# The feed-forward part's first chunk: its up tiles become a Strassen quad, with the block sums begun in rows 6 and 7

## What is computed

```
hn = rms_norm(x, g_pre_ffn)
gu = hn @ w_gate_up                       # 1024 x (2 * 2816)
hf = silu(gu[..., :2816]) * gu[..., 2816:]
ff = hf @ w_down                          # 2816 x 1024
x  = x + rms_norm(ff, g_post_ffn)
```

## Time and profile before

| what | value |
|---|---|
| median of 3 runs | 1764.18 us (1764.01 to 1764.57) |
| the profiled execution: its own time | 1763.94 us |
| its span, first to last instruction | 1762.4 us |
| TensorE busy | 1752.1 us (99%) |
| VectorE busy | 1132.3 us (64%) |
| ScalarE busy | 733.2 us (42%) |
| mean granted TensorE clock | 0.999 of full |

### The profile page before, as it was taken

One profiled execution on the slowest core, in us unless ns is written; L12 is line 12 of the kernel. 1 busy time (PEld: TensorE's weight loads), 2 busy tenths in 40 slices (PEclk: granted clock), 3 DMA queues, 4 the chain that ended last, 5 costly groups with the idle time before them and its releaser, 6 DMA issues.

```text
span 1762.4 us, 23988 instructions
## 1 busy us (share of the span) xinstructions
PE 1752.1 (99%) x8497; PEld 1453.7 (82%) x8497; DVE 1132.3 (64%) x1927; ACT 733.2 (42%) x1486; POOL 249.7 (14%) x555
## 2 busy tenths in 40 slices
PE   9999999999999999999999999999999999999998
PEld 7888888888888888888888888888888888888886
DVE  5328888888775774443555655776656655567676
ACT  5316666666643233343221123343333333344553
POOL 3321222222210001111100112101011000000011
PEclk9999999999999999999999999999999999999999
DMA  7421222222143223337635712223233322673443
GB/s 244 144 85 57 76 74 73 73 73 72 49 144 95 72 66 130 104 102 259 219 132 167 240 60 83 96 96 142 93 111 109 105 89 102 228 279 100 145 143 126
DMA packets 138047, 213.80 MB, mean 121 GB/s; under 512 B 7569, under 2 KB 94097, under 8 KB 136930
## 3 DMA queue, kind: packets, MB, share of 16 engines
q1 hardware_dynamic: 109200, 108.54, 19.6%
q0 software_dynamic: 28752, 104.04, 16.2%
q10 hardware_dynamic: 2, 0.00, 0.0%
HBM read 150.17 MB, written 62.39 MB: 121 GB/s over the span
## 4 chain that ended last, share of the span: by engine, by line
PE 98%; DVE 1%; ACT 1%; DMA 0%; issue 0%; POOL 0%; POOLq 0%; DVEq 0%; ACTq 0%
PE ps L2343 26%; PE ps L2678 22%; PE ps L2546 17%; PE ps L2734 12%; PE ps L2427 10%; PE ps L2351 3%; PE ps L2443 3%; PE ps L2465 2%; PE ps L2467 1%; DVE ring L1564 0%; DMA x_tile<-in_x_dram 0%; ACT e_t L1089 0%; ACT ring L968 0%; DVE e_t L1667 0%; DVE d_op L1564 0%
## 5 line engine op out<-in xcount | busy, mean ns | idle before, releaser
L2734 PE MATMUL ps<-d_op 128*128 128x512 f32 x924 | 210.3, 389 | 0.1
L2734 PEld LDWEIGHTS ps<-d_op 128*128 128x128 f32 x924 | 173.3, 188 | 36.8 <-DVE d_op L1564 0.5
L2678 PE MATMUL ps<-s_op,t_op_T 128*128 128x512 f32 x720 | 169.9, 389 | 0.0
L2427 PE MATMUL ps<-xn,ring 128*128 128x512 f32 x672 | 167.0, 398 | 0.0
L2678 PEld LDWEIGHTS ps<-s_op,t_op_T 128*128 128x128 f32 x720 | 135.1, 188 | 28.1
L2427 PEld LDWEIGHTS ps<-xn,ring 128*128 128x128 f32 x672 | 122.3, 188 | 24.2
L2546 PE MATMUL ps<-s_op,x_op_T 128*128 128x512 f32 x576 | 135.9, 389 | 0.0
L2546 PEld LDWEIGHTS ps<-s_op,x_op_T 128*128 128x128 f32 x576 | 108.1, 188 | 22.5
L2678 PE MATMUL ps<-hn,t_op_B 128*128 128x512 f32 x480 | 115.1, 389 | 0.0
L2678 PEld LDWEIGHTS ps<-hn,t_op_B 128*128 128x128 f32 x480 | 90.1, 188 | 18.7
L1676 DVE CUSTOM_DVE_ANT_0 ps<-ps,mask 128x256 f32<-128x256 f32 (+7 forms) x128 | 94.5, 780 | 12.2 <-PE ps L2443 11.1
(11 more groups left out here) (270 smaller groups left out, 3361.4 us busy)
## 6 DMA issues: line engine op xcount, KB each, us to landing
pair<-in_w_gate_up_dram SPq DMA_DIRECT2D x20, 1024.0 KB, 5.2
rf_pieces<-s_scratch SPq DMA_DIRECT2D x74, 256.0 KB, 2.6
x_pair<-in_w_in_dram SPq DMA_DIRECT2D x16, 1024.0 KB, 6.7
raw<-in_w_in_dram SPq DMA_DIRECT2D x26, 512.0 KB, 4.0
s_scratch<-gated_ff POOLq DMA_DIRECT2D x40, 256.0 KB, 2.5
gate_in<-gate_scratch POOLq DMA_DIRECT2D x18, 512.0 KB, 3.6
v_scratch<-v_out POOLq DMA_DIRECT2D x32, 256.0 KB, 2.6
vh<-v_scratch POOLq DMA_DIRECT2D x16, 512.0 KB, 5.1
```

What stands on the lines that cost most here:

```text
L2427: last = pe.matmul(ps[:, proj_bank(first, half), :], proj_weights(which, par, a)[:, P * k:P * (k + 1)], xn[:, b, k, HALF * half:HALF * (ha ...
L2678: last = pe.matmul(ps[:, bank, :], t_op[name][:, a, k, :], block(b, k), start=opens and (k, a, b) == (0, HH, HH), stop=(k, a, b) == (3, LL ...
L2734: last = pe.matmul(ps[:, DOWN_BANKS[product][i], :], d_op[:, g % 4, a, P * i:P * (i + 1)], d_op[:, g % 4, 2 + b, :], start=opens and (a, b ...
```

## The change

The first chunk's four direct up groups go (`GROUPS = G_FFN + 4`); a kind-1 quad stands in their place, the first of 21. The first chunk's gate groups stay, in the order tile 0, tile 1 of the first half, then of the second, and their silu goes straight into `gated_ff`. The DRAM detour, `first_sums`, the `silu` and `hf_raw` tiles go; POOL stores chunk 0 as any other. VectorE adds hn's blocks earlier: `w00` in row 6, `w10` and 256 columns of a third block in row 7, 128 and 384 columns behind row 7, the last columns behind the last row; `w00` and `w10` are new places. The residual loop on VectorE is written out in place of a hardware loop. SP loads pair 1 first, pair 0 behind the fourth block sum. In the first quad TensorE waits for `s_lo` 1, 2 and 3 ahead of T3, T2 and T1; `s_lo` 4 is made behind that quad, on ScalarE and VectorE alike. The waits of the down part's loads count one store more.

```diff
+        w10 = at("w10", [P, 4, HALF], F32, RF + 24576)
         pair = [at(f"pair{b}", [P, KT, 2 * P], F32, (RF + 24576, RRAW)[b]) for b in range(2)]
         b1_copy = at("b1_copy", [P, HALF], F32, RRING)
...
-        QUADS = 2 * (FC - 1)
+        QUADS = 2 * FC - 1
...
             load(tile_of(w_gate_up, 0))
-            load(tile_of(w_gate_up, FF))
+            load(tile_of(w_gate_up, P))
...
-            sp.wait_ge(m_lo, TT)
+            sp.wait_ge(w_lo, n.at())
+            load_pair(1, True, FF)
+            sp.wait_ge(s_summed, 4)
             load_pair(0, True, 2 * P)
-            load(tile_of(w_gate_up, P))
-            load(tile_of(w_gate_up, P + FF))
-            sp.wait_ge(w_lo, n.at())
-            load_pair(1, True, 2 * P + FF)
+            load_pair(1, False, 2 * P + FF)
...
-            pool.wait_ge(first_stored, 32)
-            pool.wait_ge(groups_done, GROUPS)
-            for f in range(2):
-                pool.dma_start(grid[:, HH, 2 * f:2 * f + 2, 1],
-                               h0_dram[P * f:P * (f + 1), :].rearrange("p (h t) -> p h t", h=2)).then_inc(first_again[0], 16)
...
-            store_chunk(1)
-            for name, j in (("S1", 3), ("S3", 1), ("S2", 0), ("S4", 2)):
-                pool.dma_start(s_dram[S_ROW[name], 0:P, :], grid[:, HH, j, 1]).then_inc(first_again[1], 16)
-            with turns(pool, FC - 2, {hidden: 4, made_n: 4}) as it:
-                store_chunk(it + 2)
+            store_chunk(0)
+            with turns(pool, FC - 1, {hidden: 4, made_n: 4}) as it:
+                store_chunk(it + 1)
...
-            def silu_half(half):
+            def first_gate(f, half):
                 act.wait_ge(groups_done, g.at(1))
-                act.activation(silu[:, HALF * half:HALF * (half + 1)], ps[:, g.slot(4), :], ACT.Silu)\
-                    .then_inc(evacuated[g.slot(4)], 1)
+                act.activation(gated_part(f, half), ps[:, g.slot(4), :], ACT.Silu).then_inc(evacuated[g.slot(4)], 1)
                 g.next()
...
-                if kind == 1:
+                if kind == 1 and not first:
                     silu_of(1, 1).then_inc(silu_ready, 1)
...
-                if kind == 1:
+                if kind == 1 and not first:
                     act.wait_ge(s_stored["S4"], chunk.at() * 16 + 16)
                     silu_of(1, 0, ps[:, BANKS[0][0], :]).then_inc(last_gate_read, 1)
...
                 wait_evacuated(act, g, half - 2)
-            silu_half(0)
-            g.next()
-            silu_half(1)
-            split_next()
-            g.next()
+            first_gate(0, 0)
+            first_gate(1, 0)
+            act.wait_ge(s_summed, 1)
+            s_hi_of(3)
+            act.wait_ge(pair_landed[1], 16)
+            t_hi_of("T3", 1, True)
+            t_hi_of("B11", 1)
+            first_gate(0, 1)
+            t_hi_of("B21", 1)
+            t_hi_of("T2", 1, True)
             act.wait_ge(s_summed, 2)
-            s_hi_of(3)
             s_hi_of(1)
-            split_next()
+            first_gate(1, 1)
             act.wait_ge(s_summed, 3)
             s_hi_of(2)
-            act.wait_ge(pair_landed[0], 16)
-            t_hi_of("T3", 0, True)
-            t_hi_of("B11", 0)
-            for half in range(2):
-                wait_evacuated(act, g, half - 2)
-            for half in range(2):
-                silu_half(half)
-                if half == 0:
-                    act.wait_ge(s_summed, 4)
-                    s_hi_of(4)
-            t_hi_of("B21", 0)
-            t_hi_of("T2", 0, True)
-            t_hi_of("T4", 0, True)
-            g.next(2)
-            ff_quad(0, first=True)
+            t_hi_of("T4", 1, True)
+            for j in range(4):
+                wait_evacuated(act, g, j - 4)
+            act.sem_inc(silu_ready, 3)
+            act.sem_inc(last_gate_read, 1)
+            act.wait_ge(s_summed, 4)
+            ff_quad(1, first=True)
+            s_hi_of(4)
+            ff_quad(0)
             ff_quad(1)
             with turns(act, FC - 3, {pr: 14, quad: 2, chunk: 1, sums_n: 8}):
                 for kind in range(2):
...
-            def whole(dst, a, kh, half):
-                s = slice(HALF * half, HALF * (half + 1))
+            def whole(dst, a, kh, half, col=0, cols=HALF):
+                s = slice(HALF * half + col, HALF * half + col + cols)
                 did(dve.tensor_tensor(dst, a[:, HH, 4 * kh:4 * kh + 4, s].bitcast(F32),
                                       a[:, LL, 4 * kh:4 * kh + 4, s].bitcast(F32), ALU.add))
...
+            def hn_whole_rows(n):
+                dve.wait_ge(tr_free[0], TT + HEADS * TT + n)
+                dve.wait_ge(tr_free[1], TT + HEADS * (TT + TT // 2) + n)
             def residual(b, i, first=False, last=False):
                 if not last:
                     merged_lo(i + 1)
+                if i == TT - 2:
+                    dve.wait_ge(m_lo, TT)
+                    hn_whole_rows(4)
+                    whole(w00[:, :, :], hn, 0, 0)
+                if last:
+                    whole(w10[:, :, :], hn, 1, 0)
+                    dve.wait_ge(groups_done, G_FFN)
+                    hn_whole_rows(6)
+                    whole(s_raw[1][:, LL, :, 0:2 * P], hn, 0, 1, 0, 2 * P)
                 if not first:
                     dve.wait_ge(tr_done[1], tile.at(tr_first))
                 dve.wait_ge(rstd_ready, tile.at() * 2 + (TT + 1))
...
-            with turns(dve, (TT - 2) // 2, {r: 2, g: 4, tile: 2, trs: 4}) as it:
+            for it in range((TT - 2) // 2):
                 residual(1, it * 2 + 1)
                 residual(0, it * 2 + 2)
             split_next()
             residual(1, TT - 1, last=True)
-            dve.wait_ge(groups_done, G_FFN)
-            whole(s_raw[2][:, LL], hn, 0, 0)
+            hn_whole_rows(TT - 1)
+            whole(s_raw[1][:, LL, :, 2 * P:3 * P], hn, 0, 1, 2 * P, P)
+            whole(s_raw[1][:, HH, :, 0:3 * P], hn, 1, 1, 0, 3 * P)
             hn_lo(TT - 1)
...
-                if first:
-                    dve.wait_ge(first_stored, 32)
...
-                dve.wait_ge(first_again[0], 48)
-                did(dve.tensor_tensor(a22, a21, a22, ALU.add))
-                did(dve.tensor_tensor(a21, a11, a21, ALU.subtract))
-                did(dve.tensor_tensor(a11, a22, a11, ALU.subtract))
-                did(dve.tensor_tensor(a12, a12, a11, ALU.subtract))
...
-            g.next()
-            dve.wait_ge(tr_free[0], TT + HEADS * TT + TT)
-            dve.wait_ge(tr_free[1], TT + HEADS * (TT + TT // 2) + TT)
-            whole(s_raw[3][:, HH], hn, 0, 1)
-            s_sum(3, s_raw[2][:, LL], s_raw[3][:, HH], ALU.subtract)
-            whole(s_raw[1][:, HH], hn, 1, 1)
-            hidden(0, 1)
-            split_next()
-            s_sum(1, s_raw[3][:, HH], s_raw[1][:, HH], ALU.add)
-            dve.wait_ge(s_summed, 2)
-            s_sum(2, s_raw[1][:, LL], s_raw[2][:, LL], ALU.subtract)
-            g.next()
-            hidden(1, 1)
-            wait_evacuated(dve, g, -1)
-            dve.sem_inc(first_ready, 2)
-            split_next()
-            s_lo_of(3, 1)
-            dve.wait_ge(pair_landed[0], 16)
+            g.next(4)
+            hn_whole_rows(TT)
+            whole(s_raw[1][:, LL, :, 3 * P:HALF], hn, 0, 1, 3 * P, P)
+            s_sum(3, w00[:, :, :], s_raw[1][:, LL], ALU.subtract)
+            dve.wait_ge(pair_landed[1], 16)
             for b in range(2):
                 dve.wait_ge(x1_stored[b], 16 * TT // 2)
-            t_sum("T3", 0)
-            t_sum("T2", 0)
-            t_sum("T4", 0)
-            t_sum("T1", 0)
-            whole(s_raw[4][:, HH], hn, 1, 0)
+            t_sum("T3", 1)
+            whole(s_raw[1][:, HH, :, 3 * P:HALF], hn, 1, 1, 3 * P, P)
+            t_sum("T2", 1)
+            t_sum("T4", 1)
+            s_lo_of(3, 1)
+            t_lo_of("T3", 1)
+            t_lo_of("B11", 1)
+            dve.wait_ge(s_summed, 1)
+            s_sum(1, s_raw[1][:, LL], s_raw[1][:, HH], ALU.add)
+            dve.wait_ge(s_summed, 2)
+            s_sum(2, s_raw[1][:, LL], w00[:, :, :], ALU.subtract)
+            t_lo_of("B21", 1)
+            t_lo_of("T2", 1)
+            t_sum("T1", 1)
             dve.wait_ge(s_summed, 3)
-            s_sum(4, s_raw[4][:, HH], s_raw[2][:, LL], ALU.subtract)
-            t_lo_of("T3", 0)
-            t_lo_of("B11", 0)
-            s_lo_of(1, 2)
-            g.next(2)
-            dve.wait_ge(first_stored, 16)
-            hidden(0, 2)
+            s_sum(4, w10[:, :, :], s_raw[2][:, LL], ALU.subtract)
             dve.wait_ge(s_summed, 4)
             s_lo_of(2, 3)
-            t_lo_of("B21", 0)
-            t_lo_of("T2", 0)
-            t_lo_of("T4", 0)
-            hidden(1, 2)
-            for half in range(2):
-                wait_evacuated(dve, g, half - 2)
-            dve.sem_inc(first_ready, 2)
+            t_lo_of("T4", 1)
+            s_lo_of(1, 3)
+            ff_quad(1, first=True)
             s_lo_of(4, 4)
-            ff_quad(0, first=True)
+            ff_quad(0)
```

(65 more changed lines are left out.)

6 lines of the change are left out of this document (1 added, 5 removed).

## The result

| | kernel before | changed kernel |
|---|---|---|
| median of 10 runs | 1764.11 us (1763.42 to 1764.96) | 1768.64 us (1768.1 to 1769.72) |
| the profiled execution: own time, span | 1763.94, 1762.4 us | 1768.30, 1766.7 us |

The ratio is 1.0025, with a 95% interval of 1.0016 to 1.0033: slower by 4.5 us. The range (1764.2 to 1769.8) holds it. The likeliest case, 1766.6 with a range of its own of 1765.9 to 1767.5 and a chance of 0.62, is 2.0 too low and did not come; the first rival, in which the clock falls, stood at 1768.7 with a chance of 0.20.

A forecast was written before the change was run, and what follows sets the result against it. The prediction took TensorE, busy 99% of the span, as the bound. 2.72 us saved and 5.2 lost to waits gave +2.5, 1766.4 on the profiled execution and 1766.6 for the median; the range was 1764.2 to 1769.8.

The forecast's parts named there:

- The likeliest case: Whole kernel: 2.72 us saved and 5.2 lost to TensorE's waits give 1766.6 us (1765.9 to 1767.5), chance 0.62.
- the first rival: TensorE's clock falls to half in the stall before the third product, adding 2.1 us: 1768.7 (1767.6 to 1770.8), chance 0.20.
- list of signs: Four signs against the forecast: waits too short before 1170, waits after it, late row 7 transposes, clock leaving 1.00 early.
- the other three signs: TensorE waits under 4.5 us in all before 1170, waits after that, or row 7's transposes are late.
- The saving: TensorE: four direct groups of 24 matmuls become seven products of 12, so 12 matmuls fewer, 2.72 us.
- Direct groups end at 1142.21: TensorE's first-chunk direct groups end after 60 of 156 matmuls, at 1142.21 and not 1163.92; the quads then want operands.
- Rows 6 and 7 cost nothing: VectorE's early sums in rows 6 and 7 fit its idle time; 0.3 us to spare before TensorE needs hn's low half.
- VectorE's queue of 39 operations, s_lo(4) at 1169.1: VectorE's work from 1131.16 to s_lo(4), ahead of the first quad's third product, takes 37.9 us, ending about 1169.1.
- TensorE's waits of 0.8, 0.2 and 4.2: TensorE waits for s_lo(2) before T2, a bank copy before T1, s_lo(4) before the third product: 5.2 us in all.
- Transfers free: Loads of both pairs land in time at no cost; the second pair's late end would cost 2.1 us.
- The clock: TensorE's 4.2 us idle stretch before the third product might halve its clock: chance 0.20, cost 2.1 us.
- The clock's price, lower bound: The kernel's first nine 512-column matmuls, at 523 ns on average, bound the cost of a clock fall from below at 1 us.

The follow-up runs named there:

- experiment 7: Changed kernel with S4's high and low parts made in the first quad, plus other first-quad operations of VectorE and ScalarE reordered: 1761.78 us, ratio 0.9987 to the kernel before.
- Experiment 6: Changed kernel with w10 made behind the rows, just ahead of the sum that reads it, instead of in row 7: 1770.5 us, ratio 1.0036 to the kernel before.
- experiment 2: Changed kernel with S4's low part moved only ahead of S1 and S2, its high part into the first quad: 1765.7 us, ratio 1.0009 to the kernel before.
- experiment 5: Changed kernel with six matmuls of no use ahead of TensorE's wait for s_lo(4): 1767.8 us, ratio 1.0019 to the kernel before.
- experiment 3: Repeat of the changed kernel with S4's low part moved only ahead of S1 and S2, for more executions: 1766.52 us, ratio 1.0013 to the kernel before.
- experiment 4: Changed kernel with twelve matmuls of no use ahead of TensorE's wait for s_lo(4): 1767.05 us, ratio 1.0016 to the kernel before.

## Why the prediction held, and where it was off

The account of the queues held, the likeliest case did not: the time came out as the first rival had it, which had 0.20. By the prediction's own list of signs the forecast was wrong, since the clock left 1.00 before the kernel's end; the other three signs did not come. That the rival's 1768.7 is within 0.1 of the measured 1768.64 is in part luck: its price for the clock was 0.6 too high, and the rest of its sum about as much too low.

- **The saving**, 2.72: right. It could be had only with the waits gone (experiment 7).
- **Direct groups end at 1142.21**: 1142.43, 0.2 later; they also started 0.27 later (1128.91 against 1128.64).
- **Rows 6 and 7 cost nothing**: right. The 0.3 us to spare ahead of the second half's groups sufficed (low half's end 1131.37, no gap in the loads from 1128.91 on). Experiment 6 shows the worth of one of these sums outside of the rows: 2.4 us of start.
- **VectorE's queue of 39 operations, s_lo(4) at 1169.1**: 1169.47. s_lo(2) at 1151.1: 1151.41. The queue began 0.3 later than forecast (1131.47 against 1131.16), so the 39 operations themselves took 38.0 us for 37.9. Counting operations at the distance of their starts, with 0.12 for one that waits for its predecessor, was good to 0.1 us here. The trace of the kernel before had none of TensorE's new waits; the order in the change and its prices were enough.
- **TensorE's waits of 0.8, 0.2 and 4.2**: 0.98, 0.30 and 4.30. The profile names t_op_T for the second, but T1's low part was done by 1154.83; ScalarE's bank copy ended at 1157.09 (1156.52 + 0.57), 0.07 ahead of the weights at 1157.16, and moving the copy (with the rest of experiment 7) removed the wait.
- **Transfers free**: right. The second pair took 5.1 us to land and was there when VectorE came.
- **The clock**: this is the step that was off, most of all in its chance. I had 0.20 for the fall and 2.1 us; by the mean clock (0.998 in nine executions, 0.997 in one) it fell in all ten, and it cost 1.5. I read the kernel's end, where 4.2 us passed between the last matmul and the fall, as if a pause had to be that long. The profiles of experiments 2 and 5 show falls around pauses of 2.4 and 2.5 us between matmuls, with TensorE already at work again when the record changes, and the mean clocks of experiments 2, 3 and 5 say that it happens in a part of the executions. With the pause of 3.9 us, the changed kernel's, it fell in ten of ten, and experiment 6, with the same pause, has one execution of five that can't be told. With 1.2 us between matmuls (experiment 4) it fell in none of eleven. A single row of one fall gives the length of one pause that suffices, and no lower bound of those that do. The rule in the Trainium skill ("TensorE: Matmul & The Clock Gate", section "Why this matters for your kernels"), to leave no pauses of some microseconds between bursts of matmuls, since the clock then falls back to half, was the better guide. The changed kernel's trace agrees with it, with a pause of 3.9 us; the Trainium skill draws its line there at longer pauses than the 2.4 us at which falls were seen here, and for these the measurements decide.
- **The clock's price, lower bound**: the prediction took the kernel's first dense matmuls, 523 ns each, as matmuls at the lower clock. The record doesn't bear that out: the granted clock reads 1.00 while they run (here from 10 us on), so what makes them slow is open, and the bound of 1 us rests on nothing shown.

```profile
10.00:11.00 1.00, 1.00 (x3) 0.83 (x3) 0.80 (x1) 1.00 (x3) 0.00 (x0) 1.00 1.08 412
```

- **The direction**: a forecast of 2.5 us slower, within the 0.2% that it gave as the least that can be told, against 4.5, or 0.25% (0.16 to 0.33). Between the profiled executions 1.9 us are to be explained: 1.5 is the clock, 0.3 the later start of the groups, 0.1 the third product's delay (5.3 for 5.2).

## What to carry to other kernels

When a change takes cover away from a full engine, list that engine's queue in order up to each point that another engine waits for, price it by the distance of starts, and compare with when it is wanted. A block of work that is "also moved earlier" has to be checked for its last piece: here nine operations of use only later stood ahead of the one that TensorE wanted. And a pause of TensorE should be priced with a share of the clock's fall, not only with its own length: here, between matmuls, none in eleven executions at 1.2 us, about six in ten at 2.4 to 2.5, all ten at 3.9, and 1.5 us for each fall. Where the order can't be changed, matmuls of no use in the pause can buy that share back: twelve did in all eleven executions, six in four of eleven.

## What was not expected of the hardware

The granted clock can fall while TensorE is already at work again: 1.2 us after it resumed in experiment 2 (resumed 1167.74, record at 1168.97 by the mean of its window), 0.2 us in the changed kernel. It was back after 3.4 us at half speed in both (1173.14 and 1172.38). The same kernel with the same pause of 2.4 us between matmuls showed both outcomes (experiments 2 and 3), and in the profile of experiment 6 a pause of 2.91 us passed without a fall. What decides within one kernel these runs do not show.
